# Normalising attention's probabilities before they are turned, instead of the weighted values after

## The chip, the cores and the metric

One core of a Trainium2 chip runs the whole program. The metric is the time of one execution on the device, in microseconds (us).

## What is computed

Two residual layers over x of 1024 tokens by 1024 channels. The change lies in layer 0, in the sparse softmax attention of 8 heads of 64 channels:

```python
logits = jnp.einsum('bthd,btkhd->bthk', qb, k_sel) * dh ** -0.5
logits = logits + bias                      # relative-position bias
logits = jnp.where(valid, logits, -jnp.inf)
p = jax.nn.softmax(logits, axis=-1)
return jnp.einsum('bthk,btkhd->bthd', p, v_sel)
...
a_out = a_out.reshape(b, s, A_WIDTH) * jax.nn.silu(ag)
```

The top 256 keys of each query are picked beforehand by a lightweight indexer; the kernel keeps all keys and adds a mask to the logits. Beside attention layer 0 has chunked gated linear attention and an output projection; layer 1 is a gated recurrent block. All matrix products with weights are made as three products of a high and a low part.

## The kernel before, in words

The program is written engine by engine, with semaphores between the engines; each engine runs its list strictly in order. Attention stands in the middle of the span, about from 378 to 598 us.

The heads go in four pairs, the queries in eight blocks of 128, which makes 32 blocks n (pair n // 8, query block n % 8). Block n has (n % 8 + 1) * 128 keys. The engines walk through steps a = 0, 1, 2, ... :

- TensorE in step a: `head_logits(a)` makes the logits of both heads of block a; then, for each group of up to four key tiles of block a-1, `turn` transposes the probabilities of both heads into PSUM (line 2002, one transposition per tile and head) and `weigh` multiplies the turned ones by the values (line 2018). After the first `turn`, `spread_inverse` transposes the reciprocal row sums, spread over 64 columns per head, so that they lie as the weighted values do (line 2010). In between go filler parts (`pair_part`): quarters of the query and key projections of the next pair, 4, 4, 2, 2, 2, 2, 0, 0 parts in the steps of a group of eight. There are none after step 25. In steps 28 to 35 transpositions of the other head group's output take place (line 2031).
- ScalarE in step a: the high part of a finished projection (line 1091), the copies of the turned probabilities from PSUM (line 1108) and the exponentials of both heads of block a, in place, with their row sums (line 1097); some splittings of weights.
- VectorE in step a: if a projection half ended in the step before, its scaling (`scale_pair_result`, line 1497); then `attended(a-2)`: it copies the spread reciprocals from PSUM, or multiplies them by the head's gate (lines 1539, 1537), and multiplies the weighted values by that into `mixT` (line 1540); then the low part of the projection (line 1503), which needs ScalarE's high part; then `inverses(a-1)`: reciprocals (line 1527) and their copy spread over columns (line 1528); then `masked(a, 0)` and `masked(a, 1)`: logits plus mask with the row maximum (line 1515) and its negation (line 1521). Projection halves end in steps 0, 1, 3, 5, 8, 9, 11, 13, 16, 17, 19, 21, 24 and 25. `gate_b` in steps 28 and later multiplies the other head group (line 1552).
- GpSimd: the bias near the diagonal is added to the mask for each head (line 787); low parts of weights (lines 671 and 662), the latter in steps 26 to 33.

All 128 x 128 probability tiles are f32. `turn` waits for the exponentials of its head alone; `weigh` for ScalarE's copies.

Of the kernel before, what the change touches and what calls it, by code (L numbers as in the profile page):

```python
# [16 lines left out]
F32 = mybir.dt.float32  # L17
# [3 lines left out]
ALU = mybir.AluOpType  # L21
ACT = mybir.ActivationFunctionType

P = 128
T = 1024
D = 1024
NT = T // P
KD = D // P
HALF = 512
A_HEADS, A_DIM = 8, 64  # L30
# [55 lines left out]
def build(nc, x, x_cols, pre_cols, index_w, rel_bias, pre_norm, post_norm, even_w_in, even_gate_w2, gate_b2, even_w_out,  # L86
          odd_w_in, odd_channels, odd_w_a, odd_w_x, odd_w_out, near_buckets, out):
    ctx = ExitStack()
    KB = 1024
    BASE = 16512  # L90
    RX = 4224
    R0, R1, R2, R3 = BASE, BASE + 64 * KB, BASE + 128 * KB, BASE + 168 * KB
    R4 = R3 + 39424

    def at(name, shape, dt, offset):
        return nc.alloc_sbuf_tensor_at(name, shape, dt, offset=offset)
# [4 lines left out]
    def sem(name):  # L101
        return ctx.enter_context(nc.semaphore(name))
# [45 lines left out]
    v = at("v", [P, NT, A_HEADS * A_DIM], F32, R3 + (o1 + 3 * P) * 4 + 4 * KB)  # L148
# [48 lines left out]
    prob = at("prob", [P, 4, T], F32, R1 + 36 * KB)  # L197
# [2 lines left out]

    mixT = at("mixT", [P, KD, T], F32, R1)
    a_gate = at("a_gate", [P, T], F32, R1 + 56 * KB)
    rl_wide = at("rl_wide", [P, P], F32, R1 + 62 * KB + 512)
    rl = at("rl", [P, 2, 2, A_DIM], F32, R1 + 63 * KB)
    a_gate_0 = at("a_gate_0", [P, T], F32, R1 + 8 * KB)
    g_two = at("g_two", [P, 2, B_HEADS * B_VAL], F32, R1 + 12 * KB)
    g_back = [at(f"g_back{i}", [P, NT // 2, B_HEADS * B_VAL], F32, R2 + off * KB) for i, off in enumerate((8, 24))]
# [34 lines left out]
    ident = at("ident", [P, P], F32, R4)  # L242
# [3 lines left out]
    mx, nmx, lsum, inv = small[:, 176:180], small[:, 180:184], small[:, 30:34], small[:, 172:174]  # L246
# [10 lines left out]
    ps = ctx.enter_context(nc.psum_tensor("ps", [P, 8, HALF], F32))  # L257
# [117 lines left out]
    near_ready = sem("near_ready")  # L375
    s_full, s_masked, max_ready, exp_done = ([sem(f"{n}{e}") for e in range(2)] for n in ("s_full", "s_masked", "max_ready", "exp_done"))
    turn_full, turn_out, pv_done, out_done = sem("turn_full"), sem("turn_out"), sem("pv_done"), sem("out_done")
    rl_ready, rl_full = sem("rl_ready"), sem("rl_full")

    a_gate_in, a_gate_0_in, a_gated = [sem("a_gate_in0"), sem("a_gate_in1")], sem("a_gate_0_in"), sem("a_gated")  # L380
    b_gate_in = [sem(f"b_gate_in{j}") for j in range(KD // 2)]
# [23 lines left out]
    def odd_half(n, m, hf):  # L405

        return ODD_HALVES.index((ODD_SEQ.index((n, m)), hf))
# [34 lines left out]
    def buffer_of(n, e):  # L442

        return 2 * e + n % 2

    def column_of(n, e):

        return n % 2 * 2 + e
# [3 lines left out]
    def pieces_at(a):  # L452

        return (2 * (a - 28), 2 * (a - 28) + 1) if 28 <= a < 28 + len(B_PIECES) // 2 else (None, None)
# [9 lines left out]
    def filler(a):  # L464

        return FILLERS[a] if a < len(FILLERS) else []
# [815 lines left out]
    def _(dve):  # L1282
        steps = Tally(dve_step)

        def own(ins):

            steps(ins)
            dve.wait_ge(dve_step, steps.n)
# [49 lines left out]
        n = 0  # L1338
        for qb in QBS:
            w = (qb + 1) * P  # L1340
# [182 lines left out]
        def inverses(n):  # L1523
            c = column_of(n, 0)
            for e in range(2):
                dve.wait_ge(exp_done[e], n + 1)
            own(dve.reciprocal(inv, lsum[:, c:c + 2]))
            dve.tensor_copy(rl[:, n % 2, :, :], inv.unsqueeze(2).to_broadcast([P, 2, A_DIM])).then_inc(rl_ready, 1)

        def attended(n):  # L1530
            p, qb = divmod(n, NT)
            dve.wait_ge(rl_full, n + 1)
            dve.wait_ge(pv_done, 2 * (blocks_of[n][-1] + 1))
            toks = slice(qb * P, (qb + 1) * P)
            if p:
                dve.wait_ge(a_gate_in[qb // 4], 16 * p)
                own(dve.tensor_tensor(rl_wide[:, :], ps[:, 7, P:2 * P], a_gate[:, toks], ALU.mult))
            else:
                own(dve.tensor_copy(rl_wide[:, :], ps[:, 7, P:2 * P]))
            dve.tensor_tensor(mixT[:, p, toks], ps[:, 7, 0:P], rl_wide[:, :], ALU.mult).then_inc(out_done, 1)  # L1540

        def gate_first_pair():
            dve.wait_ge(a_gate_0_in, 16)
# [79 lines left out]
        for t in range(NT + 1):  # L1623
# [8 lines left out]
            if t:  # L1632
                u = t - 1
                dve.wait_ge(h1h_done, u + 1)
                toks = slice(u * P, (u + 1) * P)
# [80 lines left out]
        n = LRU_BLOCKS - 1  # L1716
# [26 lines left out]
    def _(pe):  # L1743
# [51 lines left out]
        def first_out(q):  # L1795

            toks = first_tokens(*FIRST[q])
            return ps[:, FIRST_BANK[q], 0:toks.stop - toks.start], toks
# [33 lines left out]
        for q in opened:  # L1832
            dst, toks = first_out(q)
            three(dst, index_weights(FIRST[q][0], KD - 1), (hH[:, KD - 1, toks], hL[:, KD - 1, toks]), KD - 1, KD).then_inc(proj_full, 1)
        pe.wait_ge(inv_ready, 2)
        for q in range(len(FIRST_OPEN), len(FIRST)):
            dst, toks = first_out(q)
# [128 lines left out]
        def pair_part(p, f, part):  # L1966

            hf, j = divmod(f, 2)
            if part == 0:
                pe.wait_ge(w_lo, C_PAIR + 2 * p + j + 1)  # L1970
                if (p, f) == (0, 0):
                    pe.wait_ge(proj_copied, copy_count("g", C_PAIR - 1, 1))
                elif (p, f) == (0, 1):
                    pe.wait_ge(st_ready, NCH - 2)
                else:
                    pe.wait_ge(pair_scaled, 4 * p + f)
            last = weights_first(PAIR_BANK(p, f), (wH[:, j], wL[:, j]), hf, ks=range(2 * part, 2 * part + 2))
            if part == 3:
                last.then_inc(proj_full, 1)

        def head_logits(n):
            p, qb = divmod(n, NT)
            toks = slice(qb * P, (qb + 1) * P)
            h, l = qkH[p % 2], qkL[p % 2]
            pe.wait_ge(proj_free, low_count("pair", p, 1 if qb < NT // 2 else 3))
            if n:
                for e in range(2):
                    pe.wait_ge(s_masked[e], n)
            both = side_by_side([head_product(e, S_BANK[e], keys(qb), (h[:, 0, toks], l[:, 0, toks]), (h[:, 1, :], l[:, 1, :]))
                                 for e in range(2)])  # L1990
            for e, ins in enumerate(both):
                ins.then_inc(s_full[e], 1)

        def turn(g):
            n, first, m = BLOCKS[g]
            for e in range(2):
                if first == 0:
                    pe.wait_ge(exp_done[e], n + 1)
                if g:
                    pe.wait_ge(turn_out, 2 * (g - 1) + e + 1)  # L2000
                for i in range(m):
                    last = pe.transpose(ps[:, TURN_BANK[e], i * P:(i + 1) * P],  # L2002
                                        prob[:, buffer_of(n, e), (first + i) * P:(first + i + 1) * P], ident[:, :])
                last.then_inc(turn_full, 1)

        def spread_inverse(n):
            pe.wait_ge(rl_ready, n + 1)
            if n:
                pe.wait_ge(out_done, n)
            pe.transpose(ps[:, 7, P:2 * P], rl[:, n % 2, :, :], ident[:, :]).then_inc(rl_full, 1)  # L2010

        def weigh(g):
            n, first, m = BLOCKS[g]
            p, qb = divmod(n, NT)
            pe.wait_ge(turn_out, 2 * g + 2)
            for i in range(m):
                kb = first + i
                both = [pe.matmul(ps[e * A_DIM:(e + 1) * A_DIM, 7, 0:P], v[:, kb, (2 * p + e) * A_DIM:(2 * p + e + 1) * A_DIM],  # L2018
                                  pT[:, e, i * P:(i + 1) * P], start=kb == 0, stop=kb == qb) for e in range(2)]
            for ins in both:  # L2020
                ins.then_inc(pv_done, 1)

        def turn_gla(i):
            j, hf = B_PIECES[i]
            pe.wait_ge(g_back_in[hf], 16)
            if i:
                pe.wait_ge(b_gated, i)
            else:
                pe.wait_ge(proj_free, low_count("pair", PAIRS - 1, 3))
            for t in range(NT // 2):  # L2030
                last = pe.transpose(ps[:, 0, t * P:(t + 1) * P], g_back[hf][:, t, j * P:(j + 1) * P], ident[:, :])
            last.then_inc(b_turned, 1)
# [7 lines left out]
        for a in range(NW + 2):  # L2040
            parts = filler(a)
            groups = blocks_of[a - 1] if 1 <= a <= NW else []
            if a < NW:
                head_logits(a)
            for i, g in enumerate(groups):
                turn(g)
                if parts:
                    pair_part(*parts.pop(0))
                if i == 0:
                    if pieces_at(a)[0] is not None:  # L2050
                        turn_gla(pieces_at(a)[0])
                    spread_inverse(a - 1)
                weigh(g)
            for part in parts:
                pair_part(*part)
            if pieces_at(a)[1] is not None:
                turn_gla(pieces_at(a)[1])
# [73 lines left out]
        for n in range(LRU_BLOCKS):  # L2131
            block_gates(n)
            first = odd_half(n, 2, 0)
# [90 lines left out]
```

## Time and profile before

| | us |
|---|---|
| median of 3 runs | 1012.36 |
| lowest, highest | 1011.97, 1012.92 |
| the profiled execution | 1012.06 |
| its span | 1010.0 |
| TensorE busy | 958.1 (95%) |
| VectorE busy | 640.5 (63%) |
| ScalarE busy | 529.8 (52%) |
| GpSimd busy | 343.2 (34%) |

PE is TensorE, PEld its weight loads, DVE VectorE, ACT ScalarE, POOL GpSimd, SP the engine that issues most transfers. Times in the timeline count from the start of the span. A matrix product's duration overlaps with that of its neighbours, so a busy TensorE is not a TensorE at its peak; what matters is where its next instruction starts. A row's bracket says how long the engine stood idle before the instruction and whose result ended that.

### The profile page before, as it was taken

How to read it: one execution, taken by the hardware profiler on the slowest of the kernel's cores; microseconds unless marked ns; L12 is line 12 of the kernel's file. 1: busy time of each engine (PE TensorE's matmuls, PEld its weight loads, DVE VectorE, ACT ScalarE, POOL GpSimd, SP SyncE). 2: the span in 40 equal slices, each digit the busy share in tenths (PEclk: the TensorE clock that was granted, in tenths of full speed). 3: DMA queues.
4: the chain of work that ended last, by engine and by line, in shares of the span. 5: the costliest groups of instructions: out<-in, count | busy, mean ns of one | idle time of the engine just before them, and what ended most of it. 6: DMA issues, size and time to landing. Idle time of an engine off the chain costs nothing.

```text
span 1010.0 us, 15060 instructions
## 1 busy us (share of the span) xinstructions
PE 958.1 (95%) x5650; PEld 780.2 (77%) x5650; DVE 640.5 (63%) x1100; ACT 529.8 (52%) x909; POOL 343.2 (34%) x437
## 2 busy tenths in 40 slices
PE   7969999999999999899999779999999999999997
PEld 5858899888777777677777658888888888888885
DVE  5328899689799835536353744675639393989252
ACT  6627777966673445535453753433445372775111
POOL 0012065267767534442231652110422131225200
PEclk9979999999999999999999999999999999999999
DMA  9551012101223342321100633222212111103052
GB/s 352 158 92 48 1 43 50 36 21 42 84 86 93 94 126 65 116 83 39 36 33 22 240 126 132 97 84 83 84 43 63 42 43 61 42 32 126 12 208 83
DMA packets 69983, 83.88 MB, mean 83 GB/s; under 512 B 3433, under 2 KB 52633, under 8 KB 69913
## 3 DMA queue, kind: packets, MB, share of 16 engines
q1 hardware_dynamic: 68496, 81.33, 25.0%
q10 hardware_dynamic: 1416, 1.63, 1.4%
q8 instruction: 43, 0.70, 0.3%
q14 instruction: 28, 0.22, 0.1%
HBM read 64.07 MB, written 18.35 MB: 82 GB/s over the span
## 4 chain that ended last, share of the span: by engine, by line
PE 57%; DVE 5%; ACT 2%; issue 2%; DMA 2%; POOL 1%; POOLq 0%; DVEq 0%; ACTq 0%
PE ps L1747 16%; PE ps L1749 15%; PE ps L1748 15%; PE ps L2018 3%; PE ps L2002 2%; PE ps L1859 1%; ACT pT L1108 1%; DMA g_two<-gla_d 1%; PE ps L1860 1%; PE ps L1861 1%; DMA gla_d<-g_two 1%; POOL g_two L775 1%; PE ps L2081 1%; DVE tmp L1616 1%; DMA raw_row<-in_even_w_out 0%
## 5 line engine op out<-in xcount | busy, mean ns | idle before, releaser
L1747 PE MATMUL ps<-hH,wH 128*128 128x512 f32 (+1 forms) x356 | 141.0, 396 | 0.9 <-DVE scaled L1497 0.9
L1748 PE MATMUL ps<-hL,wH 128*128 128x512 f32 (+1 forms) x356 | 135.6, 381 | 0.0
L1749 PE MATMUL ps<-hH,wL 128*128 128x512 f32 (+1 forms) x356 | 135.6, 381 | 0.0
L1747 PE MATMUL ps<-h1H,w_slot_H 128*128 128x512 f32 x256 | 99.8, 390 | 0.0
L1749 PE MATMUL ps<-h1H,w_slot_L 128*128 128x512 f32 x256 | 99.6, 389 | 0.0
L1748 PE MATMUL ps<-h1L,w_slot_H 128*128 128x512 f32 x256 | 99.6, 389 | 0.0
L1360 DVE TENSOR_SCALAR_CACHE_REDUCE junk<-score,cand 128x768 bf16<-128x768 f32 (+3 forms) x128 | 96.7, 810 | 1.1
L671 POOL TENSOR_TENSOR wL<-raw,wH 128x1024 fp32r<-128x1024 f32 x28 | 70.3, 2516 | 57.0 <-ACT wH L863 56.5
L668 POOL TENSOR_TENSOR w_slot_L<-raw,w_slot_H 128x1024 fp32r<-128x1024 f32 x16 | 41.3, 2580 | 125.1 <-ACT w_slot_H L859 125.1
L1747 PEld LDWEIGHTS ps<-hH,wH 128*128 128x128 f32 x356 | 67.0, 188 | 16.8 <-issue 5.2
L1747 PE MATMUL ps<-wH,hH 128*128 128x256 f32 x256 | 75.6, 295 | 2.9 <-ACT bv L949 2.3
L1749 PEld LDWEIGHTS ps<-hH,wL 128*128 128x128 f32 x356 | 67.0, 188 | 13.2
L1748 PEld LDWEIGHTS ps<-hL,wH 128*128 128x128 f32 x356 | 67.1, 189 | 10.8
L966 ACT ACTIVATE signs<-score,cand 128x1024 bf16<-128x1024 f32 x64 | 69.9, 1092 | 6.8 <-POOL cand L693 3.9
L1748 PE MATMUL ps<-wL,hH 128*128 128x256 f32 x256 | 72.8, 284 | 0.0
L1749 PE MATMUL ps<-wH,hL 128*128 128x256 f32 x256 | 72.7, 284 | 0.0
L1097 ACT ACTIVATE prob<-prob,small 128x128 f32<-128x128 f32 (+7 forms) x64 | 49.7, 777 | 38.8 <-DVE small L1521 38.7
L1108 ACT ACTIVATE pT<-ps 128x512 f32<-128x512 f32 (+3 forms) x96 | 41.8, 486 | 37.1 <-PE ps L2002 36.9
L1515 DVE CUSTOM_DVE_ANT_0 prob<-ps,score 128x384 f32<-128x384 f32 (+5 forms) x48 | 42.7, 890 | 27.2 <-POOL score L787 23.4
L1747 PEld LDWEIGHTS ps<-wH,hH 128*128 128x128 f32 x256 | 49.3, 193 | 11.3 <-issue 11.3
L1747 PEld LDWEIGHTS ps<-h1H,w_slot_H 128*128 128x128 f32 x256 | 48.1, 188 | 10.1 <-issue 0.2
L1748 PEld LDWEIGHTS ps<-h1L,w_slot_H 128*128 128x128 f32 x256 | 48.1, 188 | 10.0
(287 smaller groups left out, 2354.2 us busy)
## 6 DMA issues: line engine op xcount, KB each, us to landing
raw<-in_even_w_in SPq DMA_DIRECT2D x28, 512.0 KB, 4.1
raw<-in_odd_w_in SPq DMA_DIRECT2D x16, 512.0 KB, 3.9
xt<-in_x_cols SPq DMA_DIRECT2D x8, 512.0 KB, 8.6
xn<-in_x SPq DMA_DIRECT2D x8, 512.0 KB, 10.2
gate_d<-gst SPq DMA_DIRECT2D x16, 256.0 KB, 2.1
raw_row<-in_even_w_out SPq DMA_DIRECT2D x8, 512.0 KB, 3.4
xt<-in_x SPq DMA_DIRECT2D x8, 512.0 KB, 3.5
x_d<-xt SPq DMA_DIRECT2D x8, 512.0 KB, 2.6
```

What stands on the lines that cost most here:

```text
L668: pool.tensor_tensor(w_slot_L[s][:, :, :], raw[:, c % 2, :, :], w_slot_H[s][:, :, :].bitcast(F32), ALU.subtract).then_inc(w_lo, 1)
L671: pool.tensor_tensor(wL[:, s, :, :], raw[:, c % 2, :, :], wH[:, s, :, :].bitcast(F32), ALU.subtract).then_inc(w_lo, 1)
L966: act.activation(signs[:, 0:(qb + 1) * P], score_of(qb), ACT.Sign, bias=cand[:, col].bitcast(F32), scale=-1.0, accum_out=cnt[:, col]).then ...
L1097: act.activation(prob[:, i, 0:w], prob[:, i, 0:w], ACT.Exp, bias=nmx[:, c:c + 1], accum_out=lsum[:, c:c + 1]).then_inc(exp_done[e], 1)
L1108: act.activation(pT[:, e, 0:m * P], ps[:, TURN_BANK[e], 0:m * P], ACT.Copy).then_inc(turn_out, 1)
L1360: return steps(dve.tensor_scalar(junk1[:, j % 2, 0:(qb + 1) * P], score_of(qb), threshold, None, op, ALU.add, accum_out=dst[:, j:j + 1]))
L1515: dve.tensor_tensor_reduce(out=prob[:, i, 0:w].rearrange("p (b w) -> p b w", b=banks), in0=ps[:, b:b + banks, 0:wb], in1=mask_of(qb).rearr ...
L1747: pe.matmul(dst, lH, rH, start=k == 0, stop=False)
L1748: pe.matmul(dst, lH, rL, start=False, stop=False)
L1749: return pe.matmul(dst, lL, rH, start=False, stop=k == nk - 1)
L2002: last = pe.transpose(ps[:, TURN_BANK[e], i * P:(i + 1) * P], prob[:, buffer_of(n, e), (first + i) * P:(first + i + 1) * P], ident[:, :])
L2018: both = [pe.matmul(ps[e * A_DIM:(e + 1) * A_DIM, 7, 0:P], v[:, kb, (2 * p + e) * A_DIM:(2 * p + e + 1) * A_DIM], pT[:, e, i * P:(i + 1) * ...
```

## The change

The row sums' reciprocals are no longer spread, transposed and multiplied in at the end. VectorE multiplies the probabilities of both heads by them in place (`tensor_scalar` over the block's keys, one instruction per head, right behind the reciprocal in `inverses`), and `turn` waits for that multiplication instead of for the exponential. `spread_inverse` and the two tiles `rl` and `rl_wide` go. `attended` has one instruction instead of two. The weighted values alternate between two regions of PSUM bank 7, and the first `weigh` of a block waits until the block two before it has been read.

```diff
@@ def inverses / attended (VectorE)
             own(dve.reciprocal(inv, lsum[:, c:c + 2]))
-            dve.tensor_copy(rl[:, n % 2, :, :], inv.unsqueeze(2).to_broadcast([P, 2, A_DIM])).then_inc(rl_ready, 1)
+            w = (n % NT + 1) * P
+            for e in range(2):
+                i = buffer_of(n, e)
+                dve.tensor_scalar(prob[:, i, 0:w], prob[:, i, 0:w], inv[:, e:e + 1], None, ALU.mult).then_inc(prob_normed[e], 1)

         def attended(n):
             p, qb = divmod(n, NT)
-            dve.wait_ge(rl_full, n + 1)
             dve.wait_ge(pv_done, 2 * (blocks_of[n][-1] + 1))
             toks = slice(qb * P, (qb + 1) * P)
+            out = ps[:, 7, n % 2 * P:(n % 2 + 1) * P]
             if p:
                 dve.wait_ge(a_gate_in[qb // 4], 16 * p)
-                own(dve.tensor_tensor(rl_wide[:, :], ps[:, 7, P:2 * P], a_gate[:, toks], ALU.mult))
+                dve.tensor_tensor(mixT[:, p, toks], out, a_gate[:, toks], ALU.mult).then_inc(out_done, 1)
             else:
-                own(dve.tensor_copy(rl_wide[:, :], ps[:, 7, P:2 * P]))
-            dve.tensor_tensor(mixT[:, p, toks], ps[:, 7, 0:P], rl_wide[:, :], ALU.mult).then_inc(out_done, 1)
+                dve.tensor_copy(mixT[:, p, toks], out).then_inc(out_done, 1)
@@ def turn / spread_inverse / weigh (TensorE)
                 if first == 0:
-                    pe.wait_ge(exp_done[e], n + 1)
+                    pe.wait_ge(prob_normed[e], n + 1)
...
-        def spread_inverse(n):
-            pe.wait_ge(rl_ready, n + 1)
-            if n:
-                pe.wait_ge(out_done, n)
-            pe.transpose(ps[:, 7, P:2 * P], rl[:, n % 2, :, :], ident[:, :]).then_inc(rl_full, 1)
...
             pe.wait_ge(turn_out, 2 * g + 2)
+            if first == 0 and n >= 2:
+                pe.wait_ge(out_done, n - 1)
             for i in range(m):
                 kb = first + i
-                both = [pe.matmul(ps[e * A_DIM:(e + 1) * A_DIM, 7, 0:P], v[:, kb, (2 * p + e) * A_DIM:(2 * p + e + 1) * A_DIM],
+                both = [pe.matmul(ps[e * A_DIM:(e + 1) * A_DIM, 7, n % 2 * P:(n % 2 + 1) * P], v[:, kb, (2 * p + e) * A_DIM:(2 * p + e + 1) * A_DIM],
                                   pT[:, e, i * P:(i + 1) * P], start=kb == 0, stop=kb == qb) for e in range(2)]
@@ the steps of TensorE
-                    spread_inverse(a - 1)
```

## Rows read from the trace of the kernel before

**Rows 1.** The page's parts 1 and 4: busy time, and the last chain by engine.

```profile
PE 958.1 (95%) x5650; PEld 780.2 (77%) x5650; DVE 640.5 (63%) x1100; ACT 529.8 (52%) x909; POOL 343.2 (34%) x437
...
PE 57%; DVE 5%; ACT 2%; issue 2%; DMA 2%; POOL 1%; POOLq 0%; DVEq 0%; ACTq 0%
```

**Rows 2.** Table of windows: stretch, length, PE busy (instructions), clock, DMA share, GB/s.

```profile
510.00:520.00 10.00, 10.00 (x77) 1.00 0.19 70
```

**Rows 3.** Timeline, TensorE, step 18: start, us, engine, line, operation, shapes, count.

```profile
500.35 0.66 PE L2002 MATMUL ps<-ident,prob 128*128 128x128 f32 x4
...
502.24 0.31 PE L2010 MATMUL ps<-ident,rl 128*128 128x128 f32 x1
502.47 0.66 PE L2018 MATMUL ps<-pT,v 128*64 128x128 f32 x8
```

**Rows 4.** Timeline, VectorE, step 18.

```profile
499.74 0.69 DVE L1497 TENSOR_TENSOR scaled<-ps,inv_rms 128x512 f32<-128x512 f32 x1 [3.17 <-PE ps L1749]
500.35 0.28 DVE L1537 TENSOR_TENSOR rl_wide<-ps,a_gate 128x128 f32<-128x128 f32 x1
500.67 0.29 DVE L1540 TENSOR_TENSOR mixT<-ps,rl_wide 128x128 f32<-128x128 f32 x1
501.13 0.69 DVE L1503 SCALAR_TENSOR_TENSOR qkL<-scaled,qkH 128x512 fp32r<-128x512 f32 x1 [0.17 <-ACT qkH L1091]
501.74 0.16 DVE L1527 RECIPROCAL small<-small 128x2 f32<-128x2 f32 x1
501.93 0.23 DVE L1528 COPY rl<-small 128x128 f32<-128x128 f32 x1
```

**Rows 5.** Groups by form, VectorE: busy us, mean ns, then idle before.

```profile
L1344 DVE TENSOR_SCALAR score<-relu,wq 128x640 f32<-128x640 f32 x1 | 2.4, 2360 | 0.8 <-ACT relu L942 0.8
...
L1344 DVE TENSOR_SCALAR score<-relu,wq 128x1024 f32<-128x1024 f32 x1 | 0.8, 754 | 0.6 <-ACT relu L942 0.6
...
L1344 DVE TENSOR_SCALAR score<-relu,wq 128x384 f32<-128x384 f32 x1 | 0.4, 419 | 9.5 <-ACT relu L942 9.5
```

**Rows 6.** Timeline, steps 20 and 22: the scaling, and the turning's start.

```profile
510.33 0.69 DVE L1497 TENSOR_TENSOR scaled<-ps,inv_rms 128x512 f32<-128x512 f32 x1 [0.18 <-PE ps L1749]
...
511.30 1.09 PE L2002 MATMUL ps<-ident,prob 128*128 128x128 f32 x8
...
523.12 0.69 DVE L1497 TENSOR_TENSOR scaled<-ps,inv_rms 128x512 f32<-128x512 f32 x1 [2.25 <-PE ps L1749]
...
524.80 1.09 PE L2002 MATMUL ps<-ident,prob 128*128 128x128 f32 x8
```

**Rows 7.** Timeline, steps 23 and 24, the ones without filler in front.

```profile
528.83 1.05 ACT L1097 ACTIVATE prob<-prob,small 128x896 f32<-128x896 f32 x1
...
531.03 1.09 PE L2002 MATMUL ps<-ident,prob 128*128 128x128 f32 x8
531.13 1.23 DVE L1515 CUSTOM_DVE_ANT_0 prob<-ps,score 128x1024 f32<-128x1024 f32 x1 [0.55 <-PE ps L1861]
...
535.22 1.15 ACT L1097 ACTIVATE prob<-prob,small 128x1024 f32<-128x1024 f32 x1
...
536.75 1.09 PE L2002 MATMUL ps<-ident,prob 128*128 128x128 f32 x8
```

**Rows 8.** Timeline, the last block's turning and what stands beside it.

```profile
589.17 0.29 DVE L1537 TENSOR_TENSOR rl_wide<-ps,a_gate 128x128 f32<-128x128 f32 x1 [1.67 <-PE ps L2018]
...
590.26 2.34 POOL L662 TENSOR_TENSOR woL<-raw_row,woH 128x1024 fp32r<-128x1024 f32 x1 [1.99 <-ACT woH L846]
...
590.53 2.16 DVE L1528 COPY rl<-small 128x128 f32<-128x128 f32 x1
...
592.74 0.33 PE L2010 MATMUL ps<-ident,rl 128*128 128x128 f32 x1 [2.24 <-DVE rl L1528]
```

**Rows 9.** Table of windows, TensorE alone, same columns as rows 2.

```profile
562.00:564.00 2.00, 0.81 (x12) 0.94 0.88 298
564.00:566.00 2.00, 2.00 (x14) 0.50 0.56 217
```

More of the change, by code:

```diff
@@ L202, in build @@
     a_gate = at("a_gate", [P, T], F32, R1 + 56 * KB)
-    rl_wide = at("rl_wide", [P, P], F32, R1 + 62 * KB + 512)
-    rl = at("rl", [P, 2, 2, A_DIM], F32, R1 + 63 * KB)
     a_gate_0 = at("a_gate_0", [P, T], F32, R1 + 8 * KB)
@@ L377, in build @@
     turn_full, turn_out, pv_done, out_done = sem("turn_full"), sem("turn_out"), sem("pv_done"), sem("out_done")
-    rl_ready, rl_full = sem("rl_ready"), sem("rl_full")
+    prob_normed = [sem("prob_normed0"), sem("prob_normed1")]
     a_gate_in, a_gate_0_in, a_gated = [sem("a_gate_in0"), sem("a_gate_in1")], sem("a_gate_0_in"), sem("a_gated")
```

## The prediction

> **What bounds the kernel now.** First the page: TensorE is busy for 95% of the span and carries 57% of the chain that ended last, VectorE 63% and 5% [rows 1]. So a cost counts where TensorE waits for it. Next the table of windows: while attention has filler work between its steps, TensorE is busy all 10.00 of 10 us [rows 2]. Then the timeline, step by step. Attention runs in 33 steps; step a makes the logits of block a, turns and weighs the probabilities of block a-1, and VectorE finishes block a-2. In each group of eight, the blocks have 128 to 1024 keys. I read step 18: TensorE turns block 17 at 500.35, right behind its logits, and never waits [rows 3]. VectorE meanwhile is late, and it does no harm: it scales a projection at 499.74, finishes block 16 at 500.35 and 500.67, subtracts at 501.13 after another 0.17 us of waiting for ScalarE's copy, and reaches the reciprocal only at 501.74 and the copy that spreads it at 501.93 [rows 4]. The turning needs only the exponentials, which are long done.
>
> **The change, part by part.** The turning of block a-1 now waits for VectorE's division, which stands behind all of the above in VectorE's order. That is the whole of the loss.
>
> *Price of one division.* An in-place multiplication of f32 by a per-partition scalar has a near form in the trace, line 1344: 0.754 us for 1024 columns and 0.419 for 384 [rows 5]. That is 0.52 ns per column and 0.22 us at no width: 0.29 for 128, 0.35 for 256, 0.49 for 512, 0.62 for 768, 0.69 for 896. Two follow one another some 0.08 us closer than they last. The bounds: no dearer than 0.22 + 1.04 ns per column (half that rate), and nothing below 0.5 ns per column. I take the row. The table of fixed costs in the Trainium skill's "VectorE: DVE Perf Modes" (the TRN2 errata section) would make 1024 columns an estimated 0.59 us, 58 cycles and half the columns; it would lower each wait by 0.16 and the sum by some 3 us, to about 1032. The row of this kernel decides.
>
> *The steps with a projection result.* There are 14 of them: steps 1, 2, 4, 6 of the first group of eight, the same in the next two, then 25 and 26 (16 instructions of line 1497 less two ahead of the steps). From the scaling to the copy at line 1528, where the first division will stand, VectorE takes 501.93 - 499.74 = 2.19 us [rows 4]. Of it the attended block gives nothing back though one instruction of 0.28 goes, since the subtraction waits for ScalarE anyway, and does so from its end on [rows 4]. The turning then starts 2.19 + division + 0.06 after the scaling. In step 18 that is 2.60 against 0.61 now: TensorE stands 2.0 us. In step 17 (128 keys) 2.54 against some 0.45, an estimate, as its logits have 256 columns and not 384: 2.1. In step 20 (512 keys) 2.74 against 511.30 - 510.33 = 0.97: 1.8. In step 22 (768 keys) 2.87 against 524.80 - 523.12 = 1.68: 1.2 [rows 6]. The second head's division ends as its turn comes. Nothing covers this: the filler work is queued on TensorE behind the turning, not in front, and with the filler steps full of work nothing of the delay is caught up.
>
> *What the spread transposition gives back.* It holds TensorE from 502.24 to 502.47, 0.23 us; I take 0.2 in each step of the 32 with filler behind it (the first five of a group) and nothing where the weighing waits for ScalarE's copy anyway. The other waits for it lie in the last group, below. Its bounds are 0 and 0.4 each. The weighing's new wait for the block two before is free: that block was finished a step earlier. Two regions of the bank instead of one cost nothing.
>
> *Steps without filler (6, 7, 8 of a group).* VectorE's order is now reciprocal, two divisions, mask, and the next exponential follows the mask. By hand for steps 22 to 24: the turning of block 21 at 525.98 instead of 524.80; the second division there ends at 526.5, the mask of block 22 comes 1.0 late, its second exponential ends near 531.1 instead of 530.1, the divisions of 22 (896) end at 532.7, so that its second head turns 1.25 late (532.75 for 531.50); mask of 23 at 532.6 instead of 531.13, second exponential at 536.25 instead of 535.22, ending at 537.5; reciprocal 0.2, two divisions of 1024; the second head turns at 539.35 instead of 537.22, 2.1 us late [rows 7]. Less 0.2: 1.9 for the three steps.
>
> *Sum.* A group costs 1.9 (its first step) + 1.8 + 1.55 - 0.2 - 0.2 (steps 3 and 5, where the division is ready before the logits end) + 1.9 = 6.7. Three groups: 20.1. In the last group step 25 costs 1.9. After it there is no filler, VectorE's chain and GpSimd's weight splitting already hold TensorE up, and delays of 0.7 to 2 us there do not add up step on step, as VectorE had 1.67 us of waiting for the weighing (589.17) before the last reciprocal [rows 8]. The last turn: reciprocal 0.65 late, divisions 0.67 + 0.75, turning, ScalarE's copy: the weighing near 593.85 instead of after the spread at 592.74, where it had waited 2.24 us [rows 8]: 0.8. The sum is 20.1 + 1.9 + 0.8 = 22.8 us. The profiled run took 1012.06, its span 1010.0; the median of the runs is 1012.36, 0.3 above. 1012.06 + 22.8 = 1034.9, say **1035**. Everything behind attention shifts unchanged.
>
> *GpSimd beside the division.* The copy at 590.53 took 2.16 us instead of 0.23: GpSimd's subtraction had started at 590.26 and lasted 2.34, and the copy ended as it did [rows 8]. The same form as the division, with 640 columns, once took 2.36 instead of 0.55 [rows 5]. A division that starts behind such an instruction can wait up to 2.3 us. In the sum the last division starts before it only by some tenths; if it starts behind it, 1.9 more. The Trainium skill's "SBUF — State Buffer" (Who interferes with whom) says more than any row here: whichever of the two starts first holds the shared ports for its whole instruction. By it the divisions would in their turn hold GpSimd's bias addition back, at most 0.75 us each time; no row shows that side.
>
> **The rivals.**
> *The division hides (faster).* If VectorE had its division ready before TensorE's logits end in the 14 steps, only the gain would be left: 27 x 0.2 and some of the waits in the last group, 6 to 9 us, 1005. It decides at a start of the division under 0.6 to 1.7 us after the scaling; the rows show 2.19. Against it: VectorE runs strictly in order, and the queue in front of the reciprocal is not changed. 0.04.
> *Partly hidden.* Where the delayed TensorE finds ScalarE and the weights earlier than now, or the last group catches up wholly, each stall might be some 1.2 instead of 1.9: 1018 to 1028. 0.10.
> *The forecast*, 1028 to 1040: 0.67.
> *GpSimd holds the divisions.* Up to 0.9 us in six steps of the last group and 2 at its end, 3 more in the others: 1040 to 1044. For it: the two instructions that end together [rows 8]. 0.08.
> *TensorE's clock falls.* Where TensorE had worked 0.81 of 2 us, the granted clock went from 0.94 to 0.50 in the next 2 us, the 1.2 GHz level [rows 9]. The new stalls of 2 us stand in steps otherwise full, so that its share stays near three quarters; but steps 22 to 24 lose more. Two us at that level lose 1 us of work, and with the slices beside it I put a stretch at 1 to 2: five of them 5 to 10 us, 1040 to 1045. 0.07.
> *The division at half the rate.* 0.52 ns more per column: 0.07 to 0.4 in steps with a projection, some 2.8 in each group's last three: 13 us, 1048. Against it stands the row of line 1344 [rows 5]. 0.02.
> *The change does not do what it says*: the spread and its copies go and the divisions come in, all in plain sight of the diff; a wait met otherwise, 1012. 0.02.
>
> **How the numbers follow.** Likeliest 1035. The range must leave out 0.2: it runs from 1027 to 1044, taking in the forecast, GpSimd's rival and part of the clock's and the partly hidden one. A change under 0.2%, 2 us, is about what a measurement of this kernel cannot tell. Faster by more: 0.04; within: 0.02; slower: 0.94.
>
> **What would show it.** In the profile after: 64 multiplications of 0.29 to 0.75 us on VectorE, none of the 32 spread transpositions; line 2002's turning waiting for them, 14 times for 1.2 to 2.1 us (less in step 26) in the steps with a projection result, with the subtraction and reciprocal just in front; no wait in steps 3 and 5 of a group; 2 us lost over steps 6 to 8; the work behind attention as long as before. It is wrong if the turning starts right behind the logits in steps like 18, if the granted clock falls in the middle of the stage, or if the multiplications last far from 0.22 + 0.52 ns per column.

## The result and the profile after

The changed kernel takes 1058.05 us (median of 4 runs, 1055.89 to 1061.39) against 1012.64 for the kernel before (1011.97 to 1015.36, measured beside it). The ratio is 1.043, 95% interval 1.0395 to 1.0466. The forecast was 1035, with a range from 1027 to 1044: the sign was right, the loss is twice the forecast. The profiled execution took 1061.39 us, the slowest of the four, with a span of 1059.3, that is 49.3 above the span of the kernel before. All ratios below leave out one slow execution, 1362.32 us at a granted clock of 0.65, of the six of the kernel "divisions first"; its median counts it and would be 1022.4 without.

The page of the changed kernel: busy times, the granted clock in 40 slices, the chain by engine and by line, and the group of the turning's products.

```profile
PE 979.1 (92%) x5618; PEld 792.1 (75%) x5618; DVE 659.1 (62%) x1100; ACT 530.8 (50%) x909; POOL 344.1 (32%) x437
...
PEclk9989998999999999898989897999999999999999
...
PE 56%; DVE 7%; ACT 3%; issue 2%; POOL 0%; DVEq 0%; ACTq 0%; POOLq 0%
...
L2002 PE MATMUL ps<-ident,prob 128*128 128x128 f32 x288 | 49.5, 311 | 33.3 <-DVE prob L1529 33.1
```

TensorE's busy time rises by 21 us [rows 1] although 32 products have gone. That is the first sign of a second loss: in attention, slices 14 to 24 counted from 0, the row of the clock shows four times 8 and once 7, where it showed 9 throughout before. The last line has the loss that was forecast: TensorE stands 33.1 us in front of the turning, for the divisions at line 1529.

Step 18 in the changed kernel, VectorE, to be laid beside [rows 4]:

```profile
530.98 0.69 DVE L1495 TENSOR_TENSOR scaled<-ps,inv_rms 128x512 f32<-128x512 f32 x1 [6.10 <-PE ps L1749]
531.58 0.28 DVE L1538 TENSOR_TENSOR mixT<-ps,a_gate 128x128 f32<-128x128 f32 x1
532.36 0.69 DVE L1501 SCALAR_TENSOR_TENSOR qkL<-scaled,qkH 128x512 fp32r<-128x512 f32 x1 [0.50 <-ACT qkH L1089]
532.97 0.16 DVE L1525 RECIPROCAL small<-small 128x2 f32<-128x2 f32 x1
533.17 0.62 DVE L1529 TENSOR_SCALAR prob<-prob,small 128x256 f32<-128x256 f32 x2
```

and TensorE in the same step, to be laid beside [rows 3]:

```profile
531.32 0.34 PE L1861 MATMUL ps<-qkH,qkL 64*128 64x384 f32 x2
533.57 0.70 PE L2002 MATMUL ps<-ident,prob 128*128 128x128 f32 x4 [1.92 <-DVE prob L1529]
```

The division starts 2.19 us after the scaling, and the turning 2.59 after it instead of 0.61. The forecast had 2.19 and 2.60. Losing an instruction in `attended` gave nothing back: VectorE now waits 0.50 instead of 0.17 for ScalarE's high part.

What follows is what the forecast's sum lacked. The table of windows around steps 17 and 18 (stretch, its length, TensorE busy with its instructions, granted clock, share and rate of transfers):

```profile
520.00:522.00 2.00, 0.79 (x8) 1.00 0.00 0
522.00:524.00 2.00, 1.18 (x6) 1.00 0.38 131
524.00:526.00 2.00, 2.00 (x9) 0.56 0.00 0
526.00:528.00 2.00, 2.00 (x6) 0.59 0.00 0
528.00:530.00 2.00, 2.00 (x10) 1.00 0.17 18
...
532.00:534.00 2.00, 0.43 (x3) 1.00 0.00 0
534.00:536.00 2.00, 2.00 (x9) 0.62 0.00 0
536.00:538.00 2.00, 2.00 (x11) 0.53 0.00 0
```

In the two slices behind each wait of 2 us the clock is at 0.53 to 0.62, close to the 1.2 GHz level. In the kernel before the same steps ran at 1.00 throughout.

**Where the 49.3 us are.** I call the attention stage the stretch from the first instruction of line 1495 (1497 before) to the end of the last of line 1606, and its clock loss the sum over slices of 2 us of their length times one minus the granted clock. That sum is an upper bound of what the clock costs, as TensorE isn't always the one that is waited for. The stage took 231.7 us before, from 368.5, with a clock loss of 2.0; it takes 276.3 in the changed kernel, from 372.5, with a loss of 27.0. So 3.9 us were lost ahead of the stage, 44.6 in it, at most 25.0 of them by the clock and at least 19.6 by waits, and 0.8 behind it.

TensorE's own busy time gives another measure. The stage before (length, then busy time and instructions of PE, PEld, DVE, ACT and POOL, the granted clock, share and rate of transfers):

```profile
368.53:600.26 231.73, 209.83 (x1576) 156.60 (x1574) 119.28 (x363) 119.41 (x259) 84.01 (x93) 0.99 0.26 85
```

In the changed kernel it is 276.32 us long, with 226.09 of TensorE (row below). TensorE stood 21.9 us of the stage before and stands 50.2 after: 28.3 more of standing and 16.3 more of busy time. So the clock cost some 16 to 25 us and the waits some 20 to 28.

### The profile page after: what moved, and what is told of

Same layout as the page of the kernel before. It is cut to its first block, busy times and chain, and to the rows that moved or that the text cites. A ratio compares the mean times of both kernels' runs of the same rounds, so it can differ in the third digit from the quotient of the medians.

```text
span 1059.3 us, 14986 instructions
## 1 busy us (share of the span) xinstructions
PE 979.1 (92%) x5618; PEld 792.1 (75%) x5618; DVE 659.1 (62%) x1100; ACT 530.8 (50%) x909; POOL 344.1 (32%) x437
## 4 chain that ended last, share of the span: by engine, by line
PE 56%; DVE 7%; ACT 3%; issue 2%; POOL 0%; DVEq 0%; ACTq 0%; POOLq 0%
PE ps L1747 15%; PE ps L1748 15%; PE ps L1749 15%; PE ps L2014 4%; PE ps L2002 4%; DVE prob L1529 2%; ACT pT L1106 1%; DVE scaled L1495 1%; ACT qkH L1089 1%; PE ps L1859 1%; PE ps L2076 1%; DVE tmp L1616 0%; DVE xt L1621 0%; PE ps L1860 0%; PE ps L1861 0%
## 5 line engine op out<-in xcount | busy, mean ns | idle before, releaser
L1747 PE MATMUL ps<-hH,wH 128*128 128x512 f32 (+1 forms) x356 | 143.9, 404 | 0.9 <-DVE scaled L1495 0.9
L1749 PE MATMUL ps<-hH,wL 128*128 128x512 f32 (+1 forms) x356 | 138.0, 388 | 0.0
L1748 PE MATMUL ps<-hL,wH 128*128 128x512 f32 (+1 forms) x356 | 138.0, 388 | 0.0
L2002 PE MATMUL ps<-ident,prob 128*128 128x128 f32 x288 | 49.5, 311 | 33.3 <-DVE prob L1529 33.1
L2002 PEld LDWEIGHTS ps<-ident,prob 128*128 128x128 f32 x288 | 34.8, 155 | 49.2 <-DVE prob L1529 42.2
L785 POOL TENSOR_TENSOR score<-nearm,near 128x256 f32<-128x256 bf16 x48 | 31.9, 677 | 102.6 <-DVE small L1513 102.1
L1747 PEld LDWEIGHTS ps<-wH,hH 128*128 128x128 f32 x256 | 50.3, 196 | 12.3 <-issue 12.3
L2014 PE MATMUL ps<-pT,v 128*64 128x128 f32 x576 | 46.8, 303 | 12.8 <-ACT pT L1106 12.8
```

Source lines behind the costliest of these rows:

```text
L785: pool.tensor_tensor(dst, nearm[:, qb, NEAR - w:NEAR], near[:, p % 2 * 2 + e, NEAR - w:NEAR], ALU.add).then_inc(near_ready, 1)
L1747: pe.matmul(dst, lH, rH, start=k == 0, stop=False)
L1748: pe.matmul(dst, lH, rL, start=False, stop=False)
L1749: return pe.matmul(dst, lL, rH, start=False, stop=k == nk - 1)
L2014: both = [pe.matmul(ps[e * A_DIM:(e + 1) * A_DIM, 7, n % 2 * P:(n % 2 + 1) * P], v[:, kb, (2 * p + e) * A_DIM:(2 * p + e + 1) * A_DIM], pT ...
```

## Experiments

Each ratio is to runs of the kernel before, measured beside the experiment on the same chip; their medians were 1016.39, 1014.44 and 1015.26 us in the three groups of experiments, and 1012.64 beside the changed kernel. The stage and its clock loss come from the one profiled execution of each. The last column takes the kernel before, 231.7 less 2.0, as its zero; as the clock loss is an upper bound, it is a lower bound of what the waits cost (the four waits of 2.0 us stand there with 3.1 in all, as 4 us of that kernel's clock loss lie in the stage's last 7 us).

| kernel | median us | ratio, 95% interval | stage | clock loss | stage less loss, over before |
|---|---|---|---|---|---|
| before | 1012.64 | | 231.7 | 2.0 | 0 |
| before, again | 1015.76 | 1.0009 (0.9988 to 1.0029) | 233.0 | 5.0 | -1.7 |
| changed | 1058.05 | 1.043 (1.0395 to 1.0466) | 276.3 | 27.0 | 19.6 |
| busy in the wait | 1047.23 | 1.0285 (1.0262 to 1.0309) | 262.6 | 9.8 | 23.1 |
| half busy | 1046.19 | 1.0326 (1.0296 to 1.0357) | 261.9 | 10.2 | 22.0 |
| wait alone | 1042.2 | 1.0243 (1.022 to 1.0265) | 265.4 | 17.4 | 18.3 |
| one tile divided | 1037.39 | 1.0201 (1.0184 to 1.0218) | 257.4 | 12.1 | 15.6 |
| divisions first | 1023.27 | 1.0065 (1.0037 to 1.0093) | 241.0 | 7.7 | 3.6 |
| per head | 1017.7 | 1.0029 (1.0012 to 1.0046) | 234.4 | 6.2 | -1.5 |
| one wait | 1015.96 | 1.0016 (0.9998 to 1.0034) | 233.0 | 3.1 | 0.2 |
| four waits | 1027.63 | 1.0125 (1.0068 to 1.0181) | 243.8 | 11.0 | 3.1 |
| eight waits in pairs | 1032.79 | 1.0181 (1.0125 to 1.0237) | 252.1 | 10.1 | 12.3 |
| per head, low part later | 1018.25 | 1.0028 (1.0004 to 1.0052) | 236.3 | 9.6 | -3.0 |
| before, low part later | 1017.35 | 1.0032 (1.0005 to 1.0059) | 234.8 | 7.8 | -2.7 |

**The clock apart from the wait.** My theory after the result: the waits are as forecast, and the rest is the clock. The rival: more waiting somewhere else. TensorE was given useless work inside the waits.

```diff
+        def keep_busy(a):
+            if a > 25 or not any(at_step == a - 1 for at_step in ended.values()):
+                return
+            for i in range({4: 7, 6: 4}.get(a % NT, 8)):
+                pe.matmul(ps[:, TURN_BANK[0], :], hH[:, 0, 0:P], hH[:, 0, 0:HALF], start=True, stop=True)
...
                 head_logits(a)
+            keep_busy(a)
             for i, g in enumerate(groups):
                 turn(g)
```

> The changed kernel, with products that nobody uses put in front of the turning in the 13 steps with a projection result up to step 25: 8, 8, 7 and 4 of 512 columns, 0.23 us apart, so that TensorE works through its wait of 2.0, 1.9, 1.7 and 1.1 us instead of standing. Nothing else changes; the results are the same. Theory A (the waits are as long as forecast, some 23 us in all, and the rest of the loss is the granted clock that falls behind each wait of about 2 us): the clock stays at 1.00 behind these steps, the attention stage's clock loss (slice lengths times one minus the clock) drops from 26 to under 10 us, and the time is 1035 to 1043, 15 to 23 below the changed kernel. Theory B (the rest is more waiting, on VectorE, GpSimd or ScalarE): the time stays at 1053 to 1061, or rises.

Measured: 1047.23 us, 17 us of stage-clock loss gone, 9.8 left. The stage as a whole, first in the changed kernel, then with the work in the waits (length, then busy time and instructions of PE, PEld, DVE, ACT and POOL, the granted clock, share and rate of transfers):

```profile
372.46:648.78 276.32, 226.09 (x1544) 165.08 (x1542) 137.81 (x363) 120.38 (x259) 84.65 (x93) 0.90 0.22 71
```

```profile
372.50:635.07 262.57, 234.34 (x1633) 171.20 (x1631) 134.72 (x363) 120.41 (x259) 84.96 (x93) 0.96 0.23 75
```

Step 17 in that kernel: the turning still starts 2.54 us behind the scaling, as in the changed kernel, but it finds TensorE at work.

```profile
511.56 0.28 PE L1861 MATMUL ps<-qkH,qkL 64*128 64x256 f32 x2
511.77 2.14 PE L1998 MATMUL ps<-hH 128*128 128x512 f32 x8
513.87 0.52 PE L2008 MATMUL ps<-ident,prob 128*128 128x128 f32 x2
```

So 89 useless products made the stage 13.7 us shorter while 17.3 us of clock loss went: a microsecond of clock loss was worth some 0.8 of time. What is left without the clock is 23.1 us over before. The median of 1047 lies 4 above my expectation of 1035 to 1043. The profile shows 4 us ahead of the stage (below), and three falls remain in the last group. The first of them, worth 5.0 us of clock loss, begins right behind the turning of step 26, the one wait of 1.92 us that this edit did not fill.

**Does a shorter wait take the clock down too?** The same edit with half the products:

```diff
-            for i in range({4: 7, 6: 4}.get(a % NT, 8)):
+            for i in range({4: 3, 6: 2}.get(a % NT, 4)):
```

> As e1_busy_in_wait with half the products: 4, 4, 3 and 2, so that TensorE stands 1.1, 1.0, 1.0 and 0.6 us in the steps with a projection result instead of 2.0, 1.9, 1.7 and 1.1. The turning starts at the same time as in e1_busy_in_wait. If a wait of 1 us leaves the clock up, the time is that of e1_busy_in_wait, 1043 to 1048, and the stage's clock loss near 10 us. If any wait takes the clock down, it is 1052 to 1060 and the loss above 20.

Measured: 1046.19 us, clock loss 10.2, as much as with the waits filled whole. TensorE stands 0.88 us here in step 17, and the clock stays:

```profile
509.31 0.52 PE L2008 MATMUL ps<-ident,prob 128*128 128x128 f32 x2 [0.88 <-DVE prob L1529]
```

```profile
506.00:508.00 2.00, 2.00 (x13) 1.00 0.00 0
508.00:510.00 2.00, 1.12 (x6) 1.00 0.39 131
510.00:512.00 2.00, 2.00 (x12) 1.00 0.00 0
```

None of the thirteen shortened waits, 0.44 to 0.88 us, was followed by a fall. All three falls (580, 618 and 628 us) lie in the last group, and the first again begins at the wait of 1.92 us of step 26, which was left as it was.

**The place in VectorE's order or the division's length.** The kernel before, with the wait alone:

```diff
                 if first == 0:
                     pe.wait_ge(exp_done[e], n + 1)
+                    pe.wait_ge(rl_ready, n + 1)
```

> The kernel before, with one edit: the turning of a block also waits for the copy of its reciprocals (line 1528), that is for the point of VectorE's order at which the division stands in the changed kernel. No division is made. Theory A (the place in VectorE's order is the cause): TensorE stands 1.8, 1.8, 1.6 and 0.8 us in the steps with a projection result, and its clock falls behind most of these waits as in the changed kernel: 1036 to 1052. Theory B (the divisions' own length is the cause): under 1022.

And the changed kernel with the shortest divisions:

```diff
-            w = (n % NT + 1) * P
+            w = P
```

> The changed kernel, but only the first 128 columns of each head's probabilities are divided, so the output is not the reference's: every division takes 0.28 us, and all waits stay. Theory A: the waits in the steps with a projection result shrink by no more than 0.3 us, steps 6 to 8 of a group lose 0.5 instead of 2 us, and the clock still falls behind waits of nearly 2 us: 1040 to 1053. Theory B (length of the divisions): under 1030.

Measured: 1042.2 and 1037.39 us. A wait for an instruction that was there before, with no division in the kernel, costs 18.3 us without the clock, and its clock loss is 15 higher than before (both from its profiled execution, which took 1049.4 us and lies 7 above its median). With the divisions cut to one tile the turning starts 2.53 us behind the scaling in all 14 steps; whole divisions make it 2.53 to 2.87, and once 3.70. The length of the divisions is worth 19.6 - 15.6 = 4 us in the stage without the clock. The second kernel, whose output is not the reference's as only the first tile is divided, lies 3 us below the lower end of my expectation. Its clock fell behind three of its eight waits of 1.85 to 2.02 us (at 386, 458 and 520 us), behind none of the six shorter ones, and at 588 us behind a wait of 1.27 us in step 27. With the wait alone it fell behind six of the eight of 1.83 to 2.05 us, and behind none of the three of 1.48 and the three of 0.76.

**The order mended.** Reciprocals and divisions at the head of VectorE's step:

```diff
         for a in range(NW + 3):
+            if 0 <= a - 1 < NW:
+                inverses(a - 1)
             for p, f in ended:
...
-            if 0 <= a - 1 < NW:
-                inverses(a - 1)
             if a < NW:
                 masked(a, 0)
...
-            if first == 0 and n >= 2:
-                pe.wait_ge(out_done, n - 1)
+            if first == 0 and n:
+                pe.wait_ge(out_done, n)
```

> The changed kernel, with reciprocal and divisions at the head of VectorE's step, in front of the scaling, the attended block and the projection's low part; the weighing then waits for the attended block one step later, for the order in PSUM bank 7. Theory A: the divisions are ready when the logits end in steps 1, 2, 3, 5 and 6 of a group, a wait of some 0.5 us remains in step 4 and 1 to 2 us in steps 7 and 8; the clock stays up: 1008 to 1020. Theory B (VectorE's added work or the collisions with GpSimd cost the time wherever they stand): over 1035.

Measured: 1023.27 us, the ratio 1.0065, 3 us above the 1008 to 1020 of my theory A. All 64 divisions are still there, at their full length, so neither VectorE's added work nor GpSimd beside it is what cost 45 us. In steps 1 and 2 of a group the turning starts 0.44 and 0.61 us behind the scaling again, as in the kernel before. Step 18 of this kernel, the reciprocal and division, the scaling, and TensorE's turning:

```profile
501.25 0.17 DVE L1525 RECIPROCAL small<-small 128x2 f32<-128x2 f32 x1 [0.74 <-ACT prob L1095]
501.45 0.62 DVE L1529 TENSOR_SCALAR prob<-prob,small 128x256 f32<-128x256 f32 x2
...
503.74 0.69 DVE L1495 TENSOR_TENSOR scaled<-ps,inv_rms 128x512 f32<-128x512 f32 x1 [1.67 <-PE ps L1749]
...
504.35 0.66 PE L2002 MATMUL ps<-ident,prob 128*128 128x128 f32 x4
```

The division ends 2.3 us before the turning wants it. TensorE still waits 8.6 us for divisions, in the later steps, where two divisions stand in series behind the second exponential. So each head got its own reciprocal and division, that of the first head in the step before, that of the second at the head of the step:

```diff
+            if 0 <= a - 1 < NW:
+                inverse(a - 1, 1)
...
                 masked(a, 1)
+                inverse(a, 0)
```

> The run with the divisions first, with each head's reciprocal and division made by itself: head 0 of a block right behind the masks of that block, head 1 at the head of the next step. Theory A: what e3_divide_first still lost (9 us of the attention stage, 6 of them by the clock) was the serial reciprocal and two divisions behind the second exponential; with one division there instead of two, 0.5 to 0.75 us less in steps 4, 7 and 8 of a group, the stage is 231 to 237 us long and the time 1010 to 1017, level with the kernel before. Theory B (VectorE's added work delays the masks): no better than e3_divide_first, 1020 to 1024.

Measured: 1017.7 us, ratio 1.0029 (1.0012 to 1.0046), just above the expected 1010 to 1017, with a stage of 234.4, as expected. Its stage is 41.9 us shorter than that of the changed kernel, and it is still not faster than the kernel before. Its stage row, and that of the kernel before profiled again:

```profile
372.39:606.80 234.41, 209.38 (x1544) 153.57 (x1542) 141.64 (x395) 120.89 (x259) 84.78 (x93) 0.98 0.26 84
```

```profile
369.70:602.73 233.03, 210.91 (x1576) 157.47 (x1574) 119.58 (x363) 119.57 (x259) 84.12 (x93) 0.98 0.26 84
```

TensorE's busy time is 1.5 us less without the 32 transpositions, VectorE's 22 more.

One further try moved GpSimd's splitting of the second weights of a pair one step later (`if a == ended[p - 1, 2 + j] + 1 + j`), with its control on the kernel before:

> e6_per_head, and GpSimd splits the second of each pair's weights (2.4 us) one step later, behind the bias additions instead of in front of them, so that the masks of step 3 and the exponentials of step 4 of a group come 1.5 us earlier. Theory A: the wait that e6_per_head still has in steps 4 and 5 of a group goes, 1 to 2 us less than e6_per_head and level with or just below the kernel before. Theory B (the delayed weights stop the filler): more than e6_per_head.

> The kernel before with the same move on GpSimd alone, the control of e11_per_head_later_low. TensorE does not wait for that exponential in the kernel before, so no change within the spread of the executions is expected: 1011 to 1018.

Measured: 1018.25 us (ratio 1.0028, 1.0004 to 1.0052) and 1017.35 (1.0032, 1.0005 to 1.0059). Neither gains; both expectations of a gain or of no change fail by some 0.3%. The profiles of both have a stage 2 to 3 us longer than their starting kernel, and a fall of the clock at 430 and 428 us (3.3 and 1.7 us of clock loss). The fall begins right behind a wait of TensorE in front of its logits, 2.24 and 1.87 us long, that ends with VectorE's mask. The same wait takes 1.56 us in the kernel per head, whose clock falls there too (1.6 us), and 0.60 in the kernel before, whose clock doesn't. So the move went with a longer wait; with one profile of each, that it causes it is not shown.

**How often does a wait of 2 us take the clock down?** The wait of the second experiment, in step 17 alone (`if n == 16`), in steps 1, 9, 17 and 25 (`if n % NT == 0`), and in steps 2, 10, 18 and 26 as well (`if n % NT in (0, 1)`).

> The kernel before with the wait of e2_wait_alone for block 16 alone, that is one wait of some 1.9 us, in step 17, in a stretch otherwise full of work. If one such wait alone takes the clock down behind it, the stage grows by 1.9 for the wait and 1 to 2 for the clock: 235 to 236 us, with a stretch at the lower level behind step 17. If it takes several, close together: 233.5 us and no such stretch.

> The kernel before with the wait of e2_wait_alone in steps 1, 9, 17 and 25 only: four waits of some 2 us, 50 us apart. Waits alone: the stage grows by 4 x 1.85 less the 0.2 to 0.5 that later steps take up, to 238 to 239 us. If each wait of 2 us also takes the clock down: another 1.5 us each, 243 to 245. If a lone wait leaves it up, as in e8_one_wait, the clock loss of the stage stays at 2 to 5 us.

> As e9_four_waits, and in steps 2, 10, 18 and 26 as well, so that the waits of 2 us come in pairs some 9 us apart. Waits alone: 245 to 247 us of stage. If neighbouring waits are what takes the clock down, falls behind most of the second waits and a clock loss of 10 us or more, 250 to 256; if each wait has its own chance, twice the falls of e9_four_waits.

Measured: 1015.96 us (ratio 1.0016, 0.9998 to 1.0034) with one wait, 1027.63 with four, 1032.79 with eight. The lone wait, in the kernel with one and in the kernel with four:

```profile
496.00:498.00 2.00, 0.34 (x6) 1.00 0.00 0
498.00:500.00 2.00, 1.66 (x8) 1.00 0.40 131
500.00:502.00 2.00, 2.00 (x12) 1.00 0.00 0
```

```profile
496.00:498.00 2.00, 1.49 (x11) 1.00 0.00 0
498.00:500.00 2.00, 0.50 (x3) 0.94 0.33 90
500.00:502.00 2.00, 2.00 (x6) 0.50 0.11 41
```

Step, wait and work around it are the same in both, and the clock falls in one of them only. With four lone waits it fell after three. With eight in pairs it fell after four, one of them the first of its pair and three the second; stage and clock loss, 252.1 and 10.1 us, are those that I expected if a neighbouring wait matters, but the other kernels don't bear that out.

I counted a fall to a wait where the lower level begins within 2.5 us of the turning's start, over all kernels and steps with a projection result:

| wait in front of the turning | waits | falls |
|---|---|---|
| changed kernel, 1.92 to 2.02 us | 9 | 6 |
| wait alone, 1.83 to 2.05 | 8 | 6 |
| one tile divided, 1.85 to 2.02 | 8 | 3 |
| one wait, 2.00 | 1 | 0 |
| four waits, 2.00 to 2.05 | 4 | 3 |
| eight waits in pairs, 1.84 to 2.05 | 8 | 4 |
| busy and half busy, step 26, 1.92 | 2 | 2 |
| changed, wait alone, one tile: 1.48 to 1.70 | 9 | 1 |
| half busy, wait alone, one tile: 0.44 to 0.88 | 19 | 0 |
| changed kernel, steps 14 and 22, 1.11 | 2 | 1 |

Of the 40 waits of 1.8 to 2.05 us 24 were followed by a fall. Where two such waits stand some 9 us apart, in steps 1 and 2 of a group, a fall came behind 8 of the 16 first and 10 of the 16 second ones, so no effect of the neighbour is seen. The one fall behind 1.11 us, in step 14, begins only after a further wait of 0.69. What decides in the single case stays open; that the same step goes either way in two executions is an argument for its place in time against the work around it, and no more than that.

The length of the stage with one wait, 233.0, can't tell the 2.0 us of the wait from the 1.3 us by which the two profiles of the kernel before differ.

**The 3.9 us ahead of the stage.**

> The kernel before, unchanged, for another profile of it. The changed kernel's profile reached attention 3.9 us later than the kernel before, with a fall of the granted clock near 172 us, in a part that the change does not touch. If this belongs to the execution and not to the change, executions of the kernel before lie in two places some 4 us apart, and this profile may show the fall near 172 us; its attention stage is 231 to 233 us long either way. If the change causes it, the fall is never seen here.

Measured: 1015.76 us. The ten runs of this kernel and the 29 of the kernel before beside it lie from 1011.05 to 1017.85. The new profile of the unchanged kernel has the fall, if a short one:

```profile
172.00:174.00 2.00, 2.00 (x12) 1.00 0.00 0
174.00:176.00 2.00, 2.00 (x12) 0.52 0.29 31
176.00:178.00 2.00, 2.00 (x13) 0.63 0.93 247
```

The other profiles settle it, as no edit touches this part: of the fourteen kept, six lose 3.4 us of clock there and reach the stage at 372.2 to 372.5 us, among them the kernel before with one wait added in step 17; two lose 1.7 and reach it at 369.3 and 369.7; six have no fall and reach it at 368.5 to 369.1, among them the changed kernel with half the products (368.50). So these 3.9 us belong to the execution and not to the change. The profiled execution that the forecast was made against has no such fall.

## Why the prediction was wrong, step by step

- *The price of one division, 0.22 us plus 0.52 ns per column*: right. Two of 256 columns last 0.62 us together, of 768 columns 1.15, of 1024 columns 1.42; the sums were 0.62, 1.16 and 1.43. Half the rate is excluded, and so are the 0.59 us for 1024 columns that I had estimated from the Trainium skill's "VectorE: DVE Perf Modes" (the TRN2 errata section).
- *The start of the turning in the steps with a projection*: right within 0.01 us. Forecast 2.54, 2.60, 2.74 and 2.87 us behind the scaling; in the third group 2.54, 2.59, 2.73 and 2.87. In the first group step 6 took 3.70. In steps 25 and 26 it was 2.53 and 2.60; the sum had nothing for step 26, where TensorE stood 1.92 us.
- *The last three steps of a group, 2.1 late*: right. In the third group, where the clock stayed up, the turnings of steps 22 and 24 start 12.80 us apart against 11.95 [rows 6, 7], which with the 1.19 of step 22 makes 2.0:

```profile
563.91 1.19 PE L2002 MATMUL ps<-ident,prob 128*128 128x128 f32 x8 [1.11 <-DVE prob L1529]
...
570.16 1.10 PE L2002 MATMUL ps<-ident,prob 128*128 128x128 f32 x8
...
576.71 1.32 PE L2002 MATMUL ps<-ident,prob 128*128 128x128 f32 x8 [0.76 <-DVE prob L1529]
```

- *The gain from the spread transposition, 0.2 us a step*: half of that. In step 2, at the full clock, turning and weighing start 2.02 us apart (398.45 and 400.47); they were 2.12 apart in step 18 before [rows 3], the same work. The product took 0.23 us, but without it the weighing starts 0.32 us behind the product in front of it, where the transposition had started at 0.24.
- *The sum of the waits, 22.8 us*: right within the bounds that the runs give. The stage without the clock loss grew by 19.6, and by 23.1 and 22.0 in the two kernels in which the clock was mostly held up; TensorE's standing grew by 28.3.
- *GpSimd beside the division*: the rival's case came. In the last step the division started 0.28 us behind GpSimd's subtraction, and two divisions took 3.28 us instead of 1.43; TensorE stood 3.58 us there:

```profile
634.22 2.34 POOL L660 TENSOR_TENSOR woL<-raw_row,woH 128x1024 fp32r<-128x1024 f32 x1 [1.74 <-ACT woH L844]
634.50 3.28 DVE L1529 TENSOR_SCALAR prob<-prob,small 128x1024 f32<-128x1024 f32 x2
...
637.16 1.97 PE L2002 MATMUL ps<-ident,prob 128*128 128x128 f32 x8 [3.58 <-DVE prob L1529]
```

  In step 19 two of 384 columns took 2.56 us instead of 0.75, and that cost TensorE 0.15. In step 8 of the first group two of 1024 took 2.53, and TensorE stood 1.53 us in two parts instead of 0.76. With the 0.83 of step 6 (last section) the sum was short by some 3 to 4 us.
- *TensorE's clock*: this step failed. It stood as a rival with a chance of 0.07 and a price of 5 to 10 us, and the sum had nothing for it. It cost 16 to 25 us. I had argued that the waits stand in steps otherwise full, so that TensorE's share stays near three quarters and only steps 22 to 24 lose more. It was the other way round: steps 22 to 24 kept the clock (their like in the first two groups lost it), while steps 17, 18 and 20, full of work around a single wait, lost it. In the changed kernel eight of the fourteen waits were followed by a fall, which together have 20.3 us of the stage's 27.0 of clock loss: 1.6 to 1.7 us each where the wait stood alone in full work, nearly as much as the wait itself, 3.4 in steps 6 and 14, and 5.1 in step 26, where other waits follow. The row that I had [rows 9] came behind several waits in a row, and I read it as an effect of them all together.
- *The work behind attention as long as before*: right, 410.5 us for 409.7. The 3.9 us ahead of the stage were not to be forecast, but of those 29 runs of the kernel before 18 lie above 1013.5 us, and eight of the fourteen profiles have it, so such a fall is likely the usual case; my sum had no term for it.

Had the clock been priced at one fall for every second wait and 2.3 us a fall, the mean here (25.0 over the 11 falls of the stage), 14 x 0.5 x 2.3 = 16 us, the sum would have been 1051; with the 4 us ahead of the stage, 1055. This is worked out from the result, and was not to be had from the rows of the kernel before.

## What to carry to other kernels

A new wait is priced by where the awaited instruction stands in its engine's order, not by how long it lasts: here the queue in front of it cost TensorE 15.6 of 19.6 us (the last column of the table), and moving the same divisions to the head of the step made the stage 35.3 us shorter, of the 44.6 that it had grown. A wait that TensorE did not have before is priced twice, once for standing and once for the clock behind it: at 2 us a fall came somewhat more often than not (24 of 40) and cost nearly as much as the wait, or more where other waits followed; at 1.5 to 1.7 us it came once in nine, and below 0.9 us never. And one profile of the kernel before is one execution; its other runs say how far it may lie from the median.

## What the runs showed of the hardware

- The granted clock fell to the 1.2 GHz level behind 24 of 40 waits of 1.8 to 2.05 us in otherwise full work, behind one of nine of 1.48 to 1.70 us, and behind none of nineteen of 0.44 to 0.88 us. Of two waits of 1.11 us one was followed by a fall, after a further wait of 0.69. The shortest falls cost 1.5 to 1.7 us of clock loss, those with further waits behind them 3.4 and 5.1. Products that nobody uses, put into the waits, made the kernel faster (1047 for 1058 us).
- A fall of the clock near 172 us, in work that no edit touches, came in eight of fourteen profiled executions and was worth 1.7 or 3.4 us of clock loss.
- An in-place multiplication on VectorE of 384 or 1024 f32 columns that started behind a GpSimd subtraction ended after it: 2.56 and 3.28 us for two instead of 0.75 and 1.43. A `scalar_tensor_tensor` with both inputs in SBUF, the low part in step 6 of the first group, took 1.52 us instead of 0.69, with a GpSimd instruction of 2.04 us beside it; its 0.83 us more are the 0.83 by which this step (3.70) exceeds the others (2.87).
